# The low halves of MLA's gate weights computed by GpSimd between the stores of the powers of c, in place of VectorE, in a two-block fp32 kernel

## The reference, cut to what matters

```python
# MLA: one projection of both token sets, split into queries, latent, rope key and gate
q_dn, kv_dn, k_rope, gate = jnp.split(h @ w_in, MLA_SPLITS, axis=-1)
...
# S5: powers of the discretized eigenvalues times c (and later times b)
lam_dt = lam * dt[:, None]
lam_bar = jnp.exp(lam_dt)
powers = jnp.exp(lam_dt[None] * jnp.arange(1, S5_CHUNK + 1, dtype=jnp.float32)[:, None, None])
...
y = jnp.einsum('btgp,gsp->btgs', xs, cmat).real
```

## Time and profile before

| what | value |
|---|---|
| median of the runs | 2179.95 us (runs: 2178.85, 2179.95, 6544.97) |
| the profiled execution's own time | 2180.76 us |
| its span (first to last instruction) | 2178.9 us |
| PE busy | 2042.8 us, 94% of the span |
| DVE busy | 1327.1 us, 61% |
| ACT busy | 792.4 us, 36% |
| POOL busy | 537.4 us, 25% |
| PE's mean granted clock | 0.974 of full speed |
| the stage of the change | about 481 to 653 us of the span |

### The profile page before, as it was taken

One profiled execution on the slowest core, in us unless ns is written; L12 is line 12 of the kernel. 1 busy time (PEld: TensorE's weight loads), 2 busy tenths in 40 slices (PEclk: granted clock), 3 DMA queues, 4 the chain that ended last, 5 costly groups with the idle time before them and its releaser, 6 DMA issues.

```text
span 2178.9 us, 39743 instructions
## 1 busy us (share of the span) xinstructions
PE 2042.8 (94%) x16166; PEld 1549.7 (71%) x16166; DVE 1327.1 (61%) x1963; ACT 792.4 (36%) x1452; POOL 537.4 (25%) x579
## 2 busy tenths in 40 slices
PE   7999898998998999999989979999989999999997
PEld 6887787767784555555555647888867788888785
DVE  3357664369766878876657856888983233333334
ACT  3325543252213443444410036555544322222223
POOL 2543211310008999940001121111111000000000
PEclk9999999999999999999999989999999999999998
DMA  9231443332351232211156424999964223233321
GB/s 363 80 97 49 158 154 122 138 123 72 109 177 69 77 116 78 108 72 44 42 183 235 166 104 130 309 306 308 311 209 159 87 97 97 97 97 97 96 88 39
DMA packets 121173, 297.72 MB, mean 137 GB/s; under 512 B 11520, under 2 KB 57728, under 8 KB 114592
## 3 DMA queue, kind: packets, MB, share of 16 engines
q1 hardware_dynamic: 110528, 241.57, 33.9%
q0 software_dynamic: 10464, 53.61, 6.7%
HBM read 227.11 MB, written 68.03 MB: 135 GB/s over the span
## 4 chain that ended last, share of the span: by engine, by line
PE 82%; DVE 9%; issue 4%; ACT 3%; POOL 1%; DMA 1%; SPq 0%; ACTq 0%; DVEq 0%; POOLq 0%
PE psum L512 30%; PE psum L2754 8%; PE psum L2931 6%; PE psum L1974 6%; PE psum L2506 5%; PE psum L2469 3%; PE psum L1184 3%; PE psum L2481 3%; PE psum L2556 2%; PE psum L3101 2%; PE psum L325 2%; PE psum L3051 1%; PE psum L3160 1%; PE psum L2495 1%; PE psum L2513 1%
## 5 line engine op out<-in xcount | busy, mean ns | idle before, releaser
L512 PE MATMUL psum<-split,w_split 128*128 128x512 f32 x1632 | 371.5, 389 | 0.0
L512 PEld LDWEIGHTS psum<-split,w_split 128*128 128x128 f32 x1632 | 306.3, 188 | 63.7
L494 DVE TENSOR_TENSOR w_split<-ring,w_split 128x512 fp32r<-128x512 f32 x182 | 129.0, 709 | 307.2 <-ACT w_split L489 306.8
L489 ACT ACTIVATE w_split<-ring 128x512 fp32r<-128x512 f32 x182 | 115.0, 632 | 333.8 <-PE psum L512 330.8
L2232 POOL TENSOR_TENSOR early<-early 128x32 f32<-128x32 f32 (+6 forms) x224 | 207.0, 924 | 17.6
L2754 PE MATMUL psum<-gate,ring 128*128 128x512 f32 (+1 forms) x512 | 165.4, 486 | 1.2 <-issue 1.2
L2931 PE MATMUL psum<-h,u_w 128*128 128x256 f32 (+1 forms) x768 | 158.8, 353 | 7.9 <-DVE h L2861 5.8
L2754 PEld LDWEIGHTS psum<-gate,ring 128*128 128x128 f32 x512 | 97.2, 190 | 69.3 <-issue 62.7
L512 PE MATMUL psum<-h,w_split 128*128 128x512 f32 x552 | 133.4, 401 | 7.9 <-DVE w_split L494 7.9
L2931 PEld LDWEIGHTS psum<-h,u_w 128*128 128x128 f32 x768 | 119.7, 193 | 27.6 <-issue 11.8
L512 PE MATMUL psum<-h_split,in_w 128*128 128x512 f32 x600 | 138.8, 391 | 0.5 <-POOL in_w L501 0.5
(11 more groups left out here) (468 smaller groups left out, 3913.2 us busy)
## 6 DMA issues: line engine op xcount, KB each, us to landing
ring<-in_s_glu SPq DMA_DIRECT2D x64, 512.0 KB, 3.5
ring<-in_w_mod SPq DMA_DIRECT2D x48, 512.0 KB, 5.5
c_pow<-made_c_pow SPq DMA_DIRECT2D x32, 576.0 KB, 5.3
ring<-in_s_in SPq DMA_DIRECT2D x32, 512.0 KB, 6.8
made_b_pow<-area POOLq DMA_DIRECT2D x15, 1024.0 KB, 4.5
b_pow<-made_b_pow SPq DMA_DIRECT2D x15, 1024.0 KB, 10.3
ring<-in_w_in SPq DMA_DIRECT2D x25, 512.0 KB, 3.6
made_table<-early POOLq DMA_DIRECT2D x16, 768.0 KB, 4.9
```

The costliest lines, as they stand in the source:

```text
L489: nc.scalar.activation(rounded(buffer(u, 0)), source(u), ACT.Copy).then_inc(act_done, 1)
L494: nc.vector.tensor_tensor(rounded(buffer(u, 1)), source(u), buffer(u, 0), ALU.subtract).then_inc(dve_done, 1)
L512: ins = nc.tensor.matmul(out, rounded(buffer(u, w)[:, ks]), values(x, k), start=(first and k == 0 and n == 0), stop=(last and k == UNIT_K ...
```

## The change

The rests of tiles 3 to 19 move from DVE's queue to POOL's. `mla_w_dve` becomes `mla_w_pool`, the same instruction on the other engine, marked on POOL's semaphore. In `c_pow_pool` the rests 3 to 7 stand ahead of the loop over the power tiles; in the loop, rest 8+j stands ahead of the wait for power tile j; the rests 16 to 19 stand behind the loop. All 17 calls leave DVE's queue, and the table of power steps is written anew, with the same 48 steps: none is left behind m = 18 and 19.

```diff
-        def mla_w_dve(dve, m):
-
-            dve.wait_ge(*at("mla_w", "rounded", m))
-            nc.vector.tensor_tensor(rounded(slot_split(("mla_in", m))), slot(("mla_in", m)), slot_split(("mla_in_high", m)),
-                                    ALU.subtract).then_inc(dve_done, 1)
-            dve_count.up("mla_w", "rest", m)
+        def mla_w_pool(pool, m):
+
+            pool.wait_ge(*at("mla_w", "rounded", m))
+            nc.gpsimd.tensor_tensor(rounded(slot_split(("mla_in", m))), slot(("mla_in", m)), slot_split(("mla_in_high", m)),
+                                    ALU.subtract).then_inc(pool_done, 1)
+            pool_count.up("mla_w", "rest", m)
...
             dve.wait_ge(dve_done, dve_count.up("s5", "angle"))
-            mla_w_dve(dve, CTX_AHEAD)
             for k in range(KD):
                 h2_low_dve(dve, k)
...
             for i in range(2, STEP + 1):
-                if i == 4:
-                    mla_w_dve(dve, CTX_AHEAD + 2)
...
         def c_pow_pool(pool):
             for m in range(2):
                 parameter_load(pool, "c", m, c_in, c_loaded)
+            for m in range(CTX_AHEAD, 8):
+                mla_w_pool(pool, m)
             for m in range(LATE_C_POW):
+                mla_w_pool(pool, 8 + m)
                 pool.wait_ge(*at("s5", "c_pow", m))
                 pool.dma_start(io["c_pow"][m], c_pow_out[m % 2]).then_inc(c_stored[m % 2], 16)
                 parameter_load(pool, "c", m + 2, c_in, c_loaded)
+            for m in range(8 + LATE_C_POW, 20):
+                mla_w_pool(pool, m)
...
-        C_STEPS_BEHIND = {7: 5, 8: 5, 9: 5, 10: 3, 11: 0, 12: 0, 13: 5, 14: 4, 15: 5, 16: 5, 17: 4, 18: 4, 19: 3}
+        C_STEPS_BEHIND = {7: 6, 8: 6, 9: 6, 10: 4, 11: 0, 12: 0, 13: 6, 14: 4, 15: 6, 16: 6, 17: 4, 18: 0, 19: 0}
...
             for m in range(CTX_AHEAD + 4, 20):
-                mla_w_dve(dve, m)
                 if m == 10:
```

More of the change, by code:

```diff
@@ L2079, in s5_setup_dve @@
             dve.wait_ge(dve_done, dve_count.up())
-            mla_w_dve(dve, CTX_AHEAD + 1)
             tt(temp[2], temp[1], re, mul)
@@ L2115, in s5_setup_dve @@
                     dve.wait_ge(dve_done, dve_count.up())
-            mla_w_dve(dve, CTX_AHEAD + 3)
             for _ in range(3):
```

## The result

The changed kernel takes 2216.14 us (median of four runs; the kernel before, beside it, 2179.4 us). The ratio is 1.0174, with a 95% interval of 1.0157 to 1.0191: slower by 37 us, within the 2% that count as no change. One execution of each kernel was in a slow state (4084.76 and 6544.97 us) and is left out of the ratio. The forecast was 2217. The profiled execution took 2216.74 us, its span 2215.0.

A forecast was written before the change was run, and what follows sets the result against it. PE, busy 94% of the span, was taken as the bound. New waits of 34.6 us plus 11.7 of slow clock, less 10.0 gained, gave +36.3 on 2180.76: 2217 us, range 2209 to 2225 (chance 0.62).

The forecast's parts named there:

- The gain: At tile 6, PE's 7.07 us wait for DVE and 2.92 us of slow clock behind it go: 10.0 us.
- POOL's rest: One 128x1024 subtraction on POOL takes 2.35 us, bounds 1.28 and 2.9; the skill's page would give 2.25.
- A turn: POOL and DVE each wait for the other's instruction to end; a rest on POOL stops DVE about 2.1 us.
- Rival (a): No turns, POOL and DVE run side by side: +14.8 us, 2195.6; chance 0.10.
- rival (b): Turns only against long power steps, small setup steps slipping between: +23.9 us, 2204.7; chance 0.11.
- (c): POOL loses turns at rests 9 and 13, +38.8 us; if a rest takes 2.9, +44.4 to +47; chance 0.14.
- Rests behind stores: In POOL's queue, rests behind power tiles and stores come late; PE waits at tiles 9, 12, 13, 15, 16: 34.6 us.
- Rival (d): Only tile 6's wait goes, freed DVE having each power tile ready in time: -10.0 us, 2170.8; chance 0.01.
- The clock: PE's clock halves after waits of 3 us or more, costing 2.92 us each; four new falls, 11.7 us.

The follow-up runs named there:

- dve_lead: Kernel before, all rests still on DVE, rests 6 to 11 one place earlier in DVE's queue; 2169.02 us, ratio 0.9960; repeated 2169.21 us, 0.9962.
- dummies: Kernel before, with POOL also doing six unused two-tensor 128x1024 subtractions, timed like rests 3 to 8; 2192.89 us, ratio 1.0057.
- setup_dve: Changed kernel with rests 3 to 8 back on DVE at their old places, 9 to 19 on POOL; 2215.71 us, ratio 1.0176.
- shift1: Changed kernel with each rest from 9 on one place further ahead in POOL's queue; 2191.74 us, ratio 1.0069.
- table: Changed kernel with DVE's table of power steps altered so power tiles 4 and 7 finish before copies of PE's results; 2194.35 us, ratio 1.0084.
- shift3_table: Changed kernel with POOL's rests three places ahead in its queue, plus the power-step edit of table; 2169.66 us, ratio 0.9963.
- dummies_one: As dummies, but each of POOL's six added instructions is a product reading one tensor instead of two; 2184.22 us, ratio 1.0038.
- rest6_pool: Kernel before with rest 6 alone moved to POOL, ahead of its wait for power tile 0; ratio 0.9993.
- shift_table: Changed kernel with the edits of shift1 and table together; 2186.4 us, ratio 1.0033.
- one_input: Changed kernel with POOL's 17 rests replaced by one-tensor products with a constant, queues and waits kept; 2206.35 us, ratio 1.0131.

## Why the prediction was right, point by point

- **The gain, 10.0.** Right. Tile 6 waits no longer; dve_lead gets the same and more without POOL.
- **POOL's rest, 2.35.** Its row is below (min, median, max): 2.35 alone, 2.39 as the median; the one of 3.10 is in the setup. The estimate of 2.25 was too low. For its upper bound the prediction adds 0.33 for a turn "in rows 8", but the row there shows 1.85 - 1.28 = 0.57; the sum does not use it.

```profile
L1959 POOL TENSOR_TENSOR ring_split<-ring,ring_split x17: 2350/2393/3102, 480.7 to 669.2; 128x1024 fp32r<-128x1024 f32 x17
```

- **A turn, 2.1.** The seven held steps take 3.56 to 3.61 in place of 1.36: 2.2. The setup ended at 533.08 (forecast 533.6), power tile 0 at 541.40 (541.9). dummies shows the turns by themselves. One reading of the earlier trace rows was off: from 757.06 to POOL's end at 758.15 it is 1.09, not 0.94, so DVE's step ends 1.21 after POOL's instruction, not a full 1.36. The changed kernel shows the same (1.22). Rival (a), no turns, falls with it, and rival (b), turns against long steps alone, by the stops of 128x128 instructions in dummies. In (c), POOL neither lost the turn at rest 9 (542.82 to 542.83) nor took 2.8 us there. It was close: in setup_dve POOL's rest 9 asked at 537.10, behind a step of DVE that began at 536.80, and took 3.30. The +38.8 of (c) does not follow from its words, either: two steps of 1.36 more would be 39.0.
- **Rests behind stores.** All five waits stand where forecast. Forecast and measured, tiles 9, 12, 13, 15, 16: 5.2 and 5.25; 9.2 and 11.39; 7.6 and 7.73; 1.3 and 1.54; 11.3 and 11.44; together 34.6 and 37.3. shift1 and table show the two causes apart. Rival (d) falls.
- **The clock, mis-sized.** My sum had 11.7 for four falls less the 2.92 before tile 6, so 8.8 net. Measured: 36.7 - 37.3 + 7.1 = 6.5. The tiles behind the waits were slowed by less than 2.92 each (tile 9 took 10.43 us, tile 12 11.11, tile 6 of the kernel before 11.30), and PE lost 1.2 less around tile 10 than in the kernel before. That is also why rest 12's wait came out 2.2 longer than forecast: rest 12 itself ended at 591.48, as forecast to the tenth, and tile 11 ended at 580.14 in place of 582.3. The two errors are one, with opposite signs; the +36.3 did not come out right by all its terms. That it came so close is in part luck: PE's time lost ahead of tile 12 and its wait there trade against each other, because DVE's queue fixes when rest 12 ends. The rule behind the term, that "a wait of 3 us or more" costs 2.92 more, does not hold as said: waits of 3.2 and 3.3 us were followed by full clock in several runs (last section).
- **The share of each cause** I had not split: the two do not add up. Without the shift, shorter stops save 9.8; with the rests three places ahead, all that waits for POOL is 5.3 us.

## What to carry to other kernels

When work moves to an engine with idle time, ask first what stands ahead of it in the new queue, and behind what that one waits: here a subtraction was queued behind a wait for the very engine it relieved, and one place in the queue was worth 24 us, the engine itself little. Price a two-tensor operation on POOL as a stop of DVE for nearly its whole length (2.2 of 2.35 us here). Look for the cheaper move first: the same gain, and 9 us under the kernel before, came from issuing six of the operations one place earlier on the engine where they were. Where a wait ends at a time that another engine sets, whatever PE saves ahead of it is given back in it.

## What the runs showed of the hardware that I had not expected

- POOL's 128x1024 product of one tensor takes 2.77 us, its difference of two 2.35 to 2.39: the one with fewer inputs is slower. Issued just behind a DVE step of 1152 columns it takes 3.9.
- A two-tensor instruction of POOL stops DVE's two-tensor instructions until it has ended, also those of 128x128 (0.40 became 2.59), and a product of one tensor too (0.23 became 2.35). With one tensor on POOL's side a DVE instruction that starts with it is held by 0.7 us; later two-tensor instructions are not, but a later copy was (0.42 became 1.23).
- The same 3.2 us wait of PE before tile 10 has three outcomes. The granted clock of 0.50 that follows costs 2.9 us in the kernel before (twice), shift3_table and dummies. It stays for a shorter time and costs some 1.7 us in the changed kernel, table, dummies_one and rest6_pool. It does not come in dve_lead (twice), shift_table, shift1, setup_dve and one_input. Two kernels, run twice, each did the same both times, which is too few to exclude chance. Neither the order of work nor the moment at which the wait falls was tried as the cause. It stays open.
- A tile takes 8.38 us in a row of tiles at full clock, and took 8.65 behind the wait of 1.54 us. Behind a wait of 5.25 us it took 10.43, behind 7.1 (tile 6 of the kernel before) 11.30, behind 11.39 and 11.44 11.11 and 10.8 (35.97 for four tiles, less 3 x 8.38). In table it took 9.98 behind a wait of 11.01. That is 1.3 to 2.7 us above 8.65, and the price does not grow with the wait.
